# Head roots, branch slabs, split look-ahead and the key-norm root moved in a hand-written order of work

## The reference, cut to what matters

```
h = rms_norm(x, g);  proj = h @ w_in                       # z_rwkv | z_moba | gates
z = z_rwkv + mu * (shift_right(z_rwkv) - z_rwkv)           # r, k, v, and three low-rank inputs
kk = k*k_k / max(sqrt(sum over the head (k*k_k)^2), 1e-12) # the keys' norm
y_a = RWKV-7 scan (two chunks of 128 tokens, triangular inverses), group norm, bonus, gate
q = partial_rope(rms_norm(q, q_norm_g)); k = partial_rope(rms_norm(k, k_norm_g))   # 8 heads of 64
y_b = causal softmax attention(q, k, v)
x = x + (sigmoid(g_a) * (y_a @ w_branch_a) + sigmoid(g_b) * (y_b @ w_branch_b)) @ w_out
x = x + conv FFN(rms_norm(x))
```

## Time and profile before

| | us |
|---|---|
| median of 3 runs | 1173.65 (1173.19 to 1174.94) |
| the profiled execution, its own time | 1173.09 |
| its span (first to last instruction) | 1171.3 |
| busy: PE, DVE, ACT, POOL | 1114.7, 782.5, 597.8, 117.3 |

### The profile page before, as it was taken

The page is one execution under the profiler, slowest core; times in us unless marked ns, Lnnn a source line. Parts: engine busy times, 40 slices in busy tenths (PEclk is TensorE's granted clock), DMA queues, the critical chain, the costliest instruction groups (busy, mean ns, idle before and its releaser), DMA issues.

```text
span 1171.3 us, 18359 instructions
## 1 busy us (share of the span) xinstructions
PE 1114.7 (95%) x7620; PEld 914.5 (78%) x7620; DVE 782.5 (67%) x1255; ACT 597.8 (51%) x927; POOL 117.3 (10%) x122
## 2 busy tenths in 40 slices
PE   7898999998999999999998999999999799999997
PEld 5766878776888888888777787878878678888786
DVE  5747774758666776566666896887578868555643
ACT  6466623244555555357555764345672277345441
POOL 0304141510000000000000000012104400000000
PEclk9899999999999999999999999999999999999999
DMA  8433321113555555455423554555441245555551
GB/s 311 161 110 105 126 91 58 53 55 120 167 199 180 174 173 184 153 192 187 144 91 108 215 201 160 184 181 194 161 161 57 74 162 172 188 181 192 187 195 55
DMA packets 49668, 177.50 MB, mean 152 GB/s; under 512 B 5648, under 2 KB 6288, under 8 KB 49328
## 3 DMA queue, kind: packets, MB, share of 16 engines
q1 hardware_dynamic: 49584, 176.32, 45.0%
HBM read 175.25 MB, written 1.05 MB: 151 GB/s over the span
## 4 chain that ended last, share of the span: by engine, by line
PE 80%; DVE 11%; ACT 6%; issue 2%; POOL 1%; DMA 1%; SPq 0%; DVEq 0%; ACTq 0%
PE wps L2666 22%; PE wps L2668 21%; PE wps L2667 21%; PE tps L2655 5%; DVE wlo L1802 2%; ACT whi L1406 1%; PE tps L2896 1%; DVE arena L2026 1%; PE tps L2901 1%; PE wps L3110 1%; PE tps L2712 1%; DVE bt L2421 1%; PE tps L3076 1%; DMA x<-in_x 1%; PE tps L2873 1%
## 5 line engine op out<-in xcount | busy, mean ns | idle before, releaser
L1802 DVE TENSOR_TENSOR wlo<-raw,whi 128x1024 fp32r<-128x1024 f32 (+1 forms) x322 | 390.6, 1234 | 177.6 <-ACT whi L1406 176.5
L2666 PE MATMUL wps<-whi,a_hi 128*128 128x512 f32 (+1 forms) x1008 | 403.4, 400 | 9.0 <-DVE wlo L1802 3.8
L2668 PE MATMUL wps<-wlo,a_hi 128*128 128x512 f32 (+1 forms) x1008 | 393.5, 390 | 0.0
L2667 PE MATMUL wps<-whi,a_lo 128*128 128x512 f32 (+1 forms) x1008 | 393.4, 390 | 0.0
L1406 ACT ACTIVATE whi<-raw 128x1024 fp32r<-128x1024 f32 (+1 forms) x322 | 325.3, 1051 | 45.0 <-PE wps L2668 42.1
L2666 PEld LDWEIGHTS wps<-whi,a_hi 128*128 128x128 f32 x1008 | 191.1, 190 | 52.4 <-issue 8.3
L2668 PEld LDWEIGHTS wps<-wlo,a_hi 128*128 128x128 f32 x1008 | 190.8, 189 | 40.1
L2667 PEld LDWEIGHTS wps<-whi,a_lo 128*128 128x128 f32 x1008 | 191.4, 190 | 36.1
L2666 PE MATMUL wps<-whi,f_hi 128*128 128x512 f32 x264 | 104.8, 397 | 0.0
L2668 PE MATMUL wps<-wlo,f_hi 128*128 128x512 f32 x264 | 104.3, 395 | 0.0
L2667 PE MATMUL wps<-whi,f_lo 128*128 128x512 f32 x264 | 104.3, 395 | 0.0
(11 more groups left out here) (419 smaller groups left out, 1262.4 us busy)
## 6 DMA issues: line engine op xcount, KB each, us to landing
raw<-in_w_dn SPq DMA_DIRECT2D x22, 512.0 KB, 3.3
raw<-in_w_0dn SPq DMA_DIRECT2D x22, 512.0 KB, 3.2
raw<-in_w_1dn SPq DMA_DIRECT2D x22, 512.0 KB, 3.2
raw<-in_w_ua SPq DMA_DIRECT2D x20, 512.0 KB, 3.3
raw<-in_w_ub SPq DMA_DIRECT2D x20, 512.0 KB, 3.3
raw<-in_w_0ug SPq DMA_DIRECT2D x20, 512.0 KB, 3.4
raw<-in_w_0uu SPq DMA_DIRECT2D x20, 512.0 KB, 3.3
raw<-in_w_1ug SPq DMA_DIRECT2D x20, 512.0 KB, 3.3
```

The source lines that it names most:

```text
L1802: V.tensor_tensor(t.wlo[n % NR][:, 0:w], t.raw[n % NR][:, 0:w], t.whi[n % NH][:, 0:w].bitcast(F32), ALU.subtract).then_inc(m.done(s.dve_lo ...
L2666: T.matmul(o, xh, wh, start=first, stop=False)
L2667: T.matmul(o, xl, wh, start=False, stop=False)
L2668: mm = T.matmul(o, xh, wl, start=False, stop=last)
```

## The change

`LOOK` goes from 2 to 3 for every stream. The roots of the attention heads are made for queries and keys apart: each has a generator of its own in the background, with its root chain of 16 columns, begun after its own `take_heads`, where before one chain of 32 columns and all four norms and rotations followed in the `mv` stream. A further split is drawn before each of these two takes. The scaling of the gains (`q_gain`) moves from step 3 to step 0 of `rope_tables`. `heads_T` of the keys comes one filler earlier, and a filler stands behind it. `key_prep` gets one more `yield` between root and spread. In the second chunk's inverse the fill at level 5 goes, and the end of the gate fillers, the transposes of `yb` and the start of `branch_b` move behind `right_side` and its fill.

```diff
-LOOK = 2
+LOOK = 3
...
+    def rotate(i):
+        emit("head_roots", "m", i)
+        yield
+        for j in range(2):
+            emit("head_norm", "m", i, j)
+            emit("rotate", i, j)
+            yield
+
     for i, name in enumerate(("mq", "mk")):
         banks = whole(stream(name, 8, main))
+        split_next()
         take_heads("m", i, 0, name, name, banks)
         if i == 0:
             background.append(rope_tables())
-
-    def rotate():
-        emit("head_roots", "m")
-        yield
-        for i in range(2):
-            for j in range(2):
-                emit("head_norm", "m", i, j)
-                emit("rotate", i, j)
-                yield
-
-    background.append(rotate())
+        background.append(rotate(i))
+
...
         emit("key_root", b.name, b.free)
         b.free = (("key_sqrt",),)
+        yield
         yield
...
     qk_t = heads_T("mq", "mqT", 4, [("rotate", 0, j) for j in range(2)])
-    fill(2)
+    fill(1)
     qk_t += heads_T("mk", "mkT", 4, [("rotate", 1, j) for j in range(2)])
+    fill(1)
...
-            if l in (2, 5):
+            if l == 2 or (l == 5 and c == 0):
                 fill(1)
...
-        if c:
-            finish()
-            to_acts("yb", [(("heads_out", "m", 0), ("heads_out", "m", 1))] * 2, ybA, 4, extra=(("grp", "g3", 1),))
-            fillers.append(branch_b())
         bs = [bank(), bank()]
         emit("right_side", c, [b.name for b in bs], [b.free for b in bs])
...
         fill(1)
+        if c:
+            finish()
+            to_acts("yb", [(("heads_out", "m", 0), ("heads_out", "m", 1))] * 2, ybA, 4, extra=(("grp", "g3", 1),))
+            fillers.append(branch_b())
...
     @part
-    def head_roots(kind):
-        dve.wait_ge(*m.at("head_sums", kind, 1, 0 if kind == "m" else 1, 1))
+    def head_roots(kind, i):
+        dve.wait_ge(*m.at("head_sums", kind, i, 0 if kind == "m" else 1, 1))
         if kind == "m":
-            rsqrt(t.mrs[:, :], t.st[:, 8:40], 32, 1.0 / 64, 1e-6, "head_roots", "m")
+            rsqrt(t.mrs[:, 16 * i:16 * i + 16], t.st[:, 8 + 16 * i:24 + 16 * i], 16, 1.0 / 64, 1e-6, "head_roots", "m", i)
...
             dve.wait_ge(*m.at("moba_in"))
+            V.tensor_scalar(t.qkg[:, 0:3:2, :], t.qkg[:, 0:3:2, :], 0.125, None, ALU.mult).then_inc(m.done(s.dve_out, "q_gain"), 1)
             V.tensor_copy(posf, t.posi[:, :]).then_inc(m.done(s.dve_out, "positions"), 1)
...
-        else:
-            dve.wait_ge(*m.at("moba_in"))
-            V.tensor_scalar(t.qkg[:, 0:3:2, :], t.qkg[:, 0:3:2, :], 0.125, None, ALU.mult).then_inc(m.done(s.dve_out, "q_gain"), 1)
```

More of the change, by code:

```diff
@@ L847, in fox_norms @@
         yield
-        emit("head_roots", "f")
+        emit("head_roots", "f", 1)
         for j in range(2):
@@ L1883, in head_norm @@
         d = heads(dst[:, j, :], n)
-        dve.wait_ge(*m.at("head_roots", kind))
+        dve.wait_ge(*(m.at("head_roots", "m", i) if kind == "m" else m.at("head_roots", "f")))
         if kind == "f":
```

## The result

Over 20 executions each, the changed kernel takes 1164.98 us in the median (1158.46 to 1177.48), the kernel before 1174.31 (1172.26 to 1176.90). The ratio is 0.9918, 95% interval 0.9902 to 0.9934. The profiled execution of after took 1161.66 us (span 1159.9) against 1173.09: -11.4, where -12.8 was forecast. So there are two results. The profiled execution gained 1.4 us less than the sum.

A forecast was written before the change was run, and what follows sets the result against it. TensorE, busy 95% of the span, was taken as the bound, so gains come only where it stands still. Terms -5.3, -3.4, -3.6, -0.5 sum to -12.8: 1173.09 to 1160.3, plus 0.56 for the median, said as 1161.0; range 1156.0 to 1166.5.

The forecast's parts named there:

- Part A: Attention query and key roots and rotations: earlier work removes TensorE idles and slow clock, -5.3 us, bounds -7.0 and -0.5.
- begun at about 47.5, with VectorE busy until 51, they end near 53: GpSimd's two key rotations in attention, forecast to leave TensorE idle only 0.8 us before the keys' transposes.
- The prediction's own sign of being wrong: Forecast declared wrong if TensorE's idle for POOL (GpSimd) stays over 2 us.
- the 3.30: TensorE idle in us that the prediction placed before the attention keys' transposes at 52.62, to shrink to 0.8.
- Rival (1): `mk` stream: VectorE is full, late splits starve TensorE and key rotations stay late; saves only 1.5, time 1165, chance 0.14.
- Part B: RWKV keys: `LOOK` 3 and the yield behind the key root remove idles and slow clock, -3.4 us, bounds -6.1 and 0.
- The idle before the squares: RWKV keys: TensorE, arriving earlier, waits for ScalarE's squares before the sums of squares; a new idle of 1.2 us.
- their exponentials and the copies behind it come late by 1 to 2 us for `probs_T`, taken as 1.5: Attention heads 6 and 7: `key_mix` ahead of their row maxima delays the softmax, counted as a 1.5 us loss.
- rival (2): RWKV keys: TensorE waits over 1.8 us for squares or exponentials at 1.2 GHz; no gain there, time 1164, chance 0.13.
- Part C: Second inverse and branch slabs: slabs cover the root before `ya`, leaving 0.7 idle; -3.6 us, bounds -4.4 and -1.
- Part D: `LOOK` elsewhere: other split waits go, the last S5 state comes 1.2 later; together -0.5 us, bounds -1.7 and +1.5.
- Rival (4): Second inverse without a slab: clock could fall to 0.50 during small matmuls; slower, time up to 1184, chance 0.05.

The follow-up runs named there:

- drive_covered: Changed kernel with one slab of the input product put between the near table and the S5 drive's small matmuls; median 1163.34 us, ratio 0.9912 to before.
- experiment 9: Changed kernel with `LOOK` back at 2, run a second time for its spread; median 1162.12 us, ratio 0.9905 to before.
- slab_in_inverse: Changed kernel without the level 2 fill in the first chunk's inverse, returning a gate slab to the second's; median 1163.32 us, ratio 0.9911 to before.
- (6): Changed kernel with one 32-column root chain, all four rotations in the `mv` stream and the keys' `heads_T` at its old place; median 1162.81 us, ratio 0.9923.
- (7): Changed kernel with `yb` transposes and branch slabs again ahead of `right_side`, level 5 fill in both chunks; median 1164.06 us, ratio 0.9928 to before.
- late_look: Changed kernel with `LOOK` 2 up to the S5 mixer's second far part and 3 behind it; median 1158.20 us, ratio 0.9864 to before.
- again: Changed kernel run once more, unaltered; median 1163.79 us, ratio 0.9925 to before.
- yield_again: Kernel before with only the extra `yield` in the keys' preparation, run a second time; median 1169.54 us, ratio 0.9966 to before.

## Why the prediction was right or wrong

**The number.** Forecast 1161.0, median 1164.98, inside the range of 1156.0 to 1166.5. The forecast was worked out against one profiled execution (-12.8). Two profiled executions of the changed kernel gave -11.4 and -14.6. That the sum lies between them is in part luck: A gave less than its term in both, B more, and these errors cancel. The difference to the median lies in the long executions, which the sum has no term for.

**Part A was mis-sized under this lead: -5.3 forecast, -2.7 measured, -3.9 in the second execution.** The failing step is "begun at about 47.5, with VectorE busy until 51, they end near 53", set beside "wants the keys at about 52.5: idle 0.8 in place of 3.30". The rotations began earlier than I said (46.5), but ended at 54.3, and TensorE asked at 51.6: idle 2.43. The prediction's own sign of being wrong, an idle for POOL over 2 us, was met. Both errors come with `LOOK` 3, which I had costed in part B and D and not here. It takes away TensorE's wait of 1.46 for a split at 44.7, so that TensorE comes sooner, and it puts a fourth split beside the second key rotation, so that VectorE runs until 52.9. With `LOOK` 2 the same edits measured -5.4 once and -4.6 twice. That the first of these meets the forecast is luck: its terms were 0.8 idle before the keys and 0.5 for late splits, and the trace has none and 1.46 plus a slow first matmul. The start was also misread: the 3.30 stood before the queries' transposes.

Rival (1) names the right place, with a different cause. Its late splits did starve TensorE with `LOOK` 2 (1.46), and not with `LOOK` 3. VectorE nearly kept its pace (norms of 0.68 and 0.81, splits 0.1 longer), and it was GpSimd that it slowed. The Trainium skill (SBUF — State Buffer, Who interferes with whom) lets the instruction that issues first hold the other up until it ends. The trace agrees for GpSimd's side, 3.04 and 2.12 against 1.15; VectorE's side, 0.1 us an instruction, is small here.

**Part B was better than forecast, -5.8 for -3.4.** The idle before the squares came as worked out (1.2 forecast, 1.51 measured). The step that failed is "their exponentials and the copies behind it come late by 1 to 2 us for `probs_T`, taken as 1.5": no idle over 0.3 us stands between 100 and 161 us in the trace of after. By the marks the two waits for `wlo` gave 3.1 with their slow first matmuls, root and low stretch 4.1, and the squares took 1.6. That the look-ahead would give 2.63 was right only in company. Alone it gave 3.1 there and lost it again at the next two waits, which is the sense of rival (2), "B's idles only move", for the look-ahead without the yield; the extra yield is what kept it from happening.

**Part C was right**, -3.9 for -3.6, with an idle of 0.12 where 0.7 was said; undoing it brought the 2.66 back.

**Part D was +1.0 in one execution and -1.1 in the other, for -0.5.** The mechanism (a split ahead of the last state) was right, and its wait of 4.7 came as 5.24, 4.00, 4.57 and 4.60 in the four traces with a lead of three, no long low stretch and no other edit there. The stretch of the S5 mixer that holds it cost 3.0, 0.7, 1.6 and 1.4, where 1.2 was forecast. In the 3.0 of after the prediction had no term for two things, the low stretch at 898 at the waits of the first far part and the longer one at 919. The other waits for `wlo` gave 0.7 in the second block and 1.3 to 1.5 behind the second far part, a little more than the 1.7 forecast. The sign of D in a single trace therefore says nothing against the sum.

**Rival (4) was underrated.** I gave 0.05 to a clock that falls in the second inverse, as one thing that either happens or doesn't. In three of the ten traces of kernels with most of the change the clock did fall at the end of that inverse (for 13.7 and 10.3 us, and for 6.8 in the trace of `drive_covered`), at 3 to 6.4 us each by the marks. "15.1 us of just such work run at 1.00 now" was no proof, since it was one execution. There are further places that I did not name at all. The two drives of the S5 mixer cost 6.4 and 2.7 to 2.9 us, where the order is that of before. In the second block's attention, at 613 to 623, seven of the ten traces have 3.4 or 6.8 us of low clock at an idle of 1.29 that every trace has, or just behind it, at a cost of 0.4 to 2.0 us by the marks. Together these places account for 9 of the 11.6, 11 of the 12.1 and 16 of the 17.4 us by which the three traced long executions lie above the lowest of their kernel.

**What stays open** is why no long execution came in 87 of the kernel before, 12 of `LOOK` 3 alone and 15 of the yield alone, when 21 of 84 were long with the kernels that hold more of the change (column "over 8"). Of these three kernels there are only four traces, so a shorter fall could have been missed there. The lead of three is not needed for it (experiment 9), nor is the slab's absence from the second inverse (2), part A (6) or part C (7): each was taken away and long executions still came. The one edit that all of these kernels share is the yield, and alone it did not bring them in 15. A kernel with parts A and C and no yield was not run, nor one with the yield and `LOOK` 3 alone. So it may be the yield together with any of the others, or something that none of these edits names, such as the time at which a stretch is reached.

## What to carry over

A look-ahead and the cover of the next long chain are one decision: making TensorE early without a slab over the wait that it then meets gives nothing, and queueing work earlier on one engine has to be costed at every place where something else is queued behind it, GpSimd's work beside it included. By the marks `LOOK` 3 gives 1.5 us in part B, 0.7 in the second block and 1.3 to 1.5 behind the last scan, and costs about 1.5 in part A and 0.7 to 3.0 in the S5 mixer; `late_look` takes the last of these gains alone. A single trace is no ruler for differences of 1 to 2 us: two of the same kernel differed by 3.2. And a forecast for work that runs in narrow matmuls should be checked over many executions, since a profile of one may show neither its long stretch of low clock nor its cost.

## What was not expected of the hardware

The same 256 matmuls of 64 columns took 7.37 us at 1.00 in one execution and 11.78 in another (`slab_in_inverse`). There the granted clock fell to 0.50 (1.2 GHz) 2.4 us behind their start, and stayed there for 13.7 us through the slab that followed, with TensorE busy all the time. The low stretches at plain idles lasted 3.4 or 6.8. In the three traces with this fall it came 2.42, 2.43 and 2.62 us behind the start of the first drive and 2.5 to 2.7 behind that of the second.

An idle does not always bring a low stretch, so it is not always "paid twice" as the prediction has it: behind 2.44 before the keys' transposes the clock stayed at 1.00 in `again`, behind 3.29 before the queries' in `yield_again`. The 1.29 near 613 was met by a low stretch in seven traces and by none in the other seven.

A GpSimd sum of 64 columns went from 0.32 to 1.30 us while VectorE ran splits, and the split took 1.33 instead of 1.2.
